# Decoder layer with product-key experts: order of ACT and PE within a step, the last unit's gathers, reused query weights, and the samples' values

## The reference, cut to what matters

```
mod = silu(c) @ w_ada + b_ada                  -> shift1, scale1, gate1, shift2, scale2, gate2
h   = rmsnorm(x) * (1 + scale1) + shift1
q, k, v, B, C, hc = split(h @ w_in)
x   = x + gate1 * (concat[window_attention(q, k, v), B * conv3(C * hc)] @ w_out)
h2  = rmsnorm(x) * (1 + scale2) + shift2
sc  = (h2 @ wq) . keys                         # 8 heads, two halves of 128 keys each
experts, gates = top 16 of the 16 x 16 sums, softmax
x   = x + gate2 * sum_k gates_k * gelu(peer_u[expert_k] . h2) * peer_v[expert_k]
y   = rmsnorm(x)
```

## Time and profile before

| | us |
|---|---|
| median of 3 runs | 3291.64 (3290.68 to 3293.53) |
| the profiled execution | 3288.59 |
| its span | 3286.6 |
| PE busy (matmuls) | 1843.0 |
| DVE busy | 2033.9 |
| ACT busy | 707.4 |
| POOL busy | 2063.0 |
| mean granted TensorE clock | 0.733 |

### The profile page before, as it was taken

How to read it: one execution, slowest core, us unless ns; L and a number is a source line. 1 busy time by engine, 2 the same in 40 slices (tenths; PEclk the granted TensorE clock), 3 DMA queues, 4 the chain that set the end, 5 groups by cost and what they waited for, 6 DMA issues and landing times.

```text
span 3286.6 us, 31584 instructions
## 1 busy us (share of the span) xinstructions
PE 1843.0 (56%) x9996; PEld 858.8 (26%) x9996; DVE 2033.9 (62%) x5142; ACT 707.4 (22%) x1967; POOL 2063.0 (63%) x2211
## 2 busy tenths in 40 slices
PE   5998478786467753364444444444444444545434
PEld 2456264343222310042112112111112111212110
DVE  3334845577687675466666666666666666666663
ACT  2121212212332131111222222222222222121111
POOL 1231656666576566557777777777777777777774
PEclk8999698998678875687676776766667676566665
DMA  8826999999999999999999999999999999999997
GB/s 305 264 96 223 351 387 369 410 389 380 364 384 388 348 371 406 408 352 404 410 409 409 409 409 406 408 403 407 401 409 404 405 407 407 405 406 404 404 407 264
DMA packets 396308, 1231.64 MB, mean 375 GB/s; under 512 B 54611, under 2 KB 107839, under 8 KB 392798
## 3 DMA queue, kind: packets, MB, share of 16 engines
q0 software_dynamic: 305728, 1109.92, 85.9%
q1 hardware_dynamic: 46314, 75.12, 6.5%
q10 hardware_dynamic: 44100, 44.59, 4.1%
HBM read 1214.45 MB, written 16.04 MB: 374 GB/s over the span
## 4 chain that ended last, share of the span: by engine, by line
POOL 28%; DMA 23%; PE 15%; DVE 14%; issue 12%; DVEq 2%; ACT 2%; ACTq 1%; SPq 1%; POOLq 0%
DMA arena<-in_peer_u,eid 15%; POOL arena L480 14%; POOL arena L491 14%; DVE arena L1491 8%; DMA arena<-in_peer_v,eid 8%; PE PS L784 3%; PE PS L662 3%; PE PS L607 2%; PE PS L624 2%; PE PS L636 2%; PE PS L712 1%; DVE arena L1480 1%; ACTq L904 1%; PE PS L674 1%; SPq L293 1%
## 5 line engine op out<-in xcount | busy, mean ns | idle before, releaser
L1491 DVE CUSTOM_DVE_ANT_0 arena<-arena,PS 128x1024 f32<-128x1024 f32 x1056 | 1243.3, 1215 | 475.8 <-DMA arena<-in_peer_u,eid 310.8
L784 PE MATMUL PS<-arena 128*32 128x512 f32 x4224 | 828.3, 925 | 1174.2 <-DMA arena<-in_peer_v,eid 1051.8
L480 POOL DMA_INDIRECT arena<-in_peer_u,eid x1056 | 997.9, 945 | 542.4 <-issue 284.5
L491 POOL DMA_INDIRECT arena<-in_peer_v,eid x1056 | 1002.6, 949 | 477.6 <-issue 299.1
L784 PEld LDWEIGHTS PS<-arena 128*32 128x32 f32 x4224 | 162.9, 145 | 1641.0 <-issue 1423.6
L1502 DVE SCALAR_TENSOR_TENSOR wgt<-gex,grec,gel 128x16 f32<-128x16 f32 x66 | 15.6, 237 | 404.7 <-ACT gel L1100 404.1
L1105 ACT ACTIVATE arena<-sel,wgt 128x32 f32<-128x32 f32 x1056 | 231.0, 307 | 40.0 <-DVE wgt L1502 40.0
L624 PE MATMUL PS<-arena 128*128 128x256 f32 (+1 forms) x576 | 172.2, 454 | 23.4 <-DVE arena L1334 21.4
L761 PEld LDWEIGHTS PS<-arena 128*128 128x128 f32 x1280 | 154.7, 201 | 46.7 <-issue 42.1
L761 PE MATMUL PS<-arena 128*128 128x128 f32 x1280 | 162.3, 287 | 3.3 <-ACT arena L1090 3.3
L1095 ACT ACTIVATE arena<-PS 128x256 f32<-128x256 f32 x42 | 16.1, 384 | 666.9 <-PE PS L772 666.9
(11 more groups left out here) (237 smaller groups left out, 1967.9 us busy)
## 6 DMA issues: line engine op xcount, KB each, us to landing
arena<-in_w_ada SPq DMA_DIRECT2D x24, 1024.0 KB, 8.1
arena<-in_peer_u,eid POOLq DMA_INDIRECT x1056, 9.3
arena<-in_peer_v,eid POOLq DMA_INDIRECT x1056
arena<-in_peer_wq ACTq DMA_DIRECT2D x13, 1024.0 KB, 6.5
arena<-in_peer_wq SPq DMA_DIRECT2D x4, 2048.0 KB, 42.2
arena<-in_w_in SPq DMA_DIRECT2D x14, 512.0 KB, 8.1
arena<-in_w_in ACTq DMA_DIRECT2D x14, 512.0 KB, 15.5
arena<-in_x_prompt ACTq DMA_DIRECT2D x8, 512.0 KB, 7.4
```

The lines of the kernel that those rows point to most:

```text
L480: po.indirect_dma_start(out=Ur[:, k % RING, :], out_offset=None, in_=a["peer_u"], in_offset=bass.IndirectOffsetOnAxis(ap=eid[m % 4][:, k:k ...
L491: po.indirect_dma_start(out=Vr[:, k % RING, :], out_offset=None, in_=a["peer_v"], in_offset=bass.IndirectOffsetOnAxis(ap=eid[m % 4][:, k:k ...
L784: last = mm(PS[j * GT:(j + 1) * GT, half, :], dsel[m % 2][:, k, :], Vr[:, k % RING, half * 512:(half + 1) * 512], start=m % 2 == 0 and q = ...
L1491: last = ve.tensor_tensor_reduce(out=Ur[:, k % RING, :], in0=Ur[:, k % RING, :], in1=hP, scale=1.0, scalar=0.0, op0=ALU.mult, op1=ALU.add, ...
```

## The change

Order on ACT: `selectors` loses its Gelu, which becomes the first thing in a step. The sample exponentials move behind the next piece's evacuation and `sample_soft2` one piece on. `store_mod` moves to positions 5 and 10. One root of a constant is computed ahead of the first norm. Order on PE: pieces i + 3 and i + 4 stand between quads 1 and 2, piece i + 5 between quads 2 and 3, none behind quad 3. Gathers: the last unit's quads 0 and 1 go into the ring of u rows, quads 2 and 3 into slots of the ring of v rows. Weights: heads 5 to 7, still in the buffers from the first tile, are the first three Q pieces, so three loads are left out. Samples' values (SD): the new rows' part for all eight samples is one matmul of 128 columns in place of eight of 16.

```diff
+            def gather_last(q):
+                po.wait_ge(s["dots_done"], (UNITS - 1) * NU + 6 + 2 * q)
+                for k in range(q * VB, (q + 1) * VB):
+                    po.indirect_dma_start(
+                        out=Ur[:, k % RING, :], out_offset=None, in_=a["peer_v"],
...
+                    ).then_inc(last_ld[q], 16)
+
-            for n in range(UNITS + 1):
+            for n in range(UNITS - 1):
...
+            for q in range(NV):
+                gather_u(UNITS - 1, 2 * q)
+                gather_u(UNITS - 1, 2 * q + 1)
+                if q == NV - 1:
+                    gather_last(0)
+                gather_v(UNITS - 2, q)
+            gather_last(1)
+            for q in (2, 3):
+                po.wait_ge(s["pv_done"], (UNITS - 2) * NV + q + 1)
...
                 if kind == "SD":
                     p = n * 64
+                    mm(PS[p:p + 64, 6, 0:NS * 16], vnat[0:NSAMP, PT, p:p + 64], PTn.rearrange("p n c -> p (n c)"), start=True, stop=False)
                     for m in range(NS):
-                        mm(PS[p:p + 64, 6, m * 16:(m + 1) * 16], cVn[:, m, p:p + 64], PTc[:, m, :], start=True, stop=False)
-                        last = mm(PS[p:p + 64, 6, m * 16:(m + 1) * 16], vnat[0:NSAMP, PT, p:p + 64], PTn[:, m, :], start=False, stop=True)
+                        last = mm(PS[p:p + 64, 6, m * 16:(m + 1) * 16], cVn[:, m, p:p + 64], PTc[:, m, :], start=False, stop=m == NS - 1)
...
                 if kind == "Q":
-                    pe.wait_ge(*take(wqA_ld, PH + n))
+                    pe.wait_ge(*take(wqA_ld, PH - 3 + n))
...
             def weigh(m, q):
                 pe.wait_ge(s["diag_ready"], m + 1)
-                pe.wait_ge(v_ld[q % VBUFS], 16 * VB * ((m * NV + q) // VBUFS + 1))
+                rows = Vr
+                if m < UNITS - 1:
+                    pe.wait_ge(v_ld[q % VBUFS], 16 * VB * ((m * NV + q) // VBUFS + 1))
+                elif q < 2:
+                    pe.wait_ge(last_ld[q], 16 * VB)
+                    rows = Ur
+                else:
+                    pe.wait_ge(v_ld[q % VBUFS], 16 * VB * (m * NV // VBUFS + 1))
...
                     weigh(n - 1, 1)
-                if i + 3 < last_i:
-                    piece(i + 3)
+                for q in (3, 4):
+                    if i + q < last_i:
+                        piece(i + q)
                 if 1 <= n <= UNITS:
                     weigh(n - 1, 2)
-                if i + 4 < last_i:
-                    piece(i + 4)
+                if i + 5 < last_i:
+                    piece(i + 5)
                 if FIRST <= n + 2 < UNITS:
                     scores(n + 2)
                 if 1 <= n <= UNITS:
                     weigh(n - 1, 3)
-                if i + 5 < last_i:
-                    piece(i + 5)
...
                 last.then_inc(s["piece_ev"], 1)
+                if i and PIECES[i - 1][0] == "SB":
+                    ac.wait_ge(s["sm_done"], PIECES[i - 1][1] + 1)
+                    act_(SS, SS, ACT.Exp)
+                    act_(ses[:, :], ses[:, :], ACT.Exp).then_inc(s["se_done"], 1)
...
                     if n + 3 < PH:
-                        load_wqA(PH + n + 3)
+                        load_wqA(PH + n)
...
-                if pos in (4, 8):
-                    store_mod(pos // 4)
+                if pos in (5, 10):
+                    store_mod(pos // 5)
...
+            act_(sqw[:, :], epsb[:, :], ACT.Sqrt)
             first_squares(0)
...
-                load_wqA(h + 3)
+                if h + 3 < PH:
+                    load_wqA(h + 3)
...
+            def gelu(m):
+                ac.wait_ge(s["dots_done"], (m + 1) * NU)
+                act_(gel[:, m % 2, :], act[:, m % 2, :], ACT.Gelu).then_inc(s["gelu_done"], 1)
+
             def selectors(m):
                 par = m % 2
-                ac.wait_ge(s["dots_done"], (m + 1) * NU)
-                act_(gel[:, par, :], act[:, par, :], ACT.Gelu).then_inc(s["gelu_done"], 1)
...
+                if 1 <= n <= UNITS:
+                    gelu(n - 1)
                 left = n >= 2 and i - 1 < last_i
...
-                if before == "SB":
-                    sample_soft2(m)
+                if i >= 2 and PIECES[i - 2][0] == "SB":
+                    sample_soft2(PIECES[i - 2][1])
```

More of the change, by code:

```diff
@@ L219, in build @@
         wgt = sb("wgt", [128, 2, TOPK])
-        rin, epsb = sb("rin", [128, 5]), sb("epsb", [128, 1])
+        rin, epsb, sqw = sb("rin", [128, 5]), sb("epsb", [128, 1]), sb("sqw", [128, 1])
         tickv = sb("tickv", [128, 4])
@@ L246, in build @@
         v_ld = [sem(f"v_ld{i}") for i in range(VBUFS)]
+        last_ld = [sem(f"last_ld{i}") for i in range(2)]
         block = ctx.enter_context(nc.Block())
@@ L494, in gather_v @@
                     ).then_inc(v_ld[b % VBUFS], 16)
-            for n in range(UNITS + 1):
+            def gather_last(q):
[3 more added lines that the diff above has]
+                        out=Ur[:, k % RING, :], out_offset=None, in_=a["peer_v"],
+                        in_offset=bass.IndirectOffsetOnAxis(ap=eid[(UNITS - 1) % 4][:, k:k + 1], axis=0),
+                    ).then_inc(last_ld[q], 16)
+            for n in range(UNITS - 1):
                 for q in range(NV):
@@ L502, in _ @@
                         gather_v(n - 1, q)
+            for q in range(NV):
[7 more added lines that the diff above has]
+                po.wait_ge(s["pv_done"], (UNITS - 2) * NV + q + 1)
+                for k in range(q * VB, (q + 1) * VB):
+                    po.indirect_dma_start(
+                        out=Vr[:, k % RING, :], out_offset=None, in_=a["peer_v"],
+                        in_offset=bass.IndirectOffsetOnAxis(ap=eid[(UNITS - 1) % 4][:, k:k + 1], axis=0),
+                    ).then_inc(v_ld[q % VBUFS], 16)
         @block.tensor
@@ L607, in piece @@
                                 last = mm(PS[:, 6 + n % 2, half * 256 + (t - 1) * 128:half * 256 + t * 128],
-                                          wqA[(PH + n) % 3][:, k, half * 128:(half + 1) * 128], (h2T[1] if t == 1 else h2T2)[:, k, :],
+                                          wqA[(PH - 3 + n) % 3][:, k, half * 128:(half + 1) * 128], (h2T[1] if t == 1 else h2T2)[:, k, :],
                                           start=k == 0, stop=k == KT - 1)
@@ L783, in weigh @@
                         j = k % 4
-                        last = mm(PS[j * GT:(j + 1) * GT, half, :], dsel[m % 2][:, k, :], Vr[:, k % RING, half * 512:(half + 1) * 512],
+                        last = mm(PS[j * GT:(j + 1) * GT, half, :], dsel[m % 2][:, k, :], rows[:, k % RING, half * 512:(half + 1) * 512],
                                   start=m % 2 == 0 and q == 0, stop=m % 2 == 1 and q == NV - 1)
@@ L943, in piece @@
                 if kind == "SB":
-                    ac.wait_ge(s["sm_done"], n + 1)
-                    act_(SS, SS, ACT.Exp)
-                    act_(ses[:, :], ses[:, :], ACT.Exp).then_inc(s["se_done"], 1)
                     return
@@ L980, in piece @@
                 if kind == "Q":
-                    last = act_(qA12[:, 2 * n:2 * n + 2, :], PS[:, 6 + n % 2, :].rearrange("p (a b) -> p a b", a=2), ACT.Copy)
+                    last = act_(qA12[:, 2 * ((PH - 3 + n) % PH):2 * ((PH - 3 + n) % PH) + 2, :], PS[:, 6 + n % 2, :].rearrange("p (a b) -> p a b", a=2), ACT.Copy)
                 if kind == "W":
```

## The result

| | before, us | after, us |
|---|---|---|
| median of 4 runs | 3291.16 | 3247.84 (3242.39 to 3251.76) |
| the profiled execution | 3288.59 | 3242.39 |
| its span | 3286.6 | 3240.6 |
| first gather issued | 287.87 | 274.95 |
| first gather of unit 24 | 1478.2 | 1439.8 |

The ratio is 0.9873, with a 95% interval of 0.9859 to 0.9887: 43.3 us faster, where 31.3 were forecast. The profiled execution after is the fastest of its four, so the 46.0 us between the two spans are some 3 us more than the medians give. The gathers' start times sort these 46.0: 12.9 us before the first gather (forecast 13.7), 25.6 between the first gather and unit 24 (10), none from there to the last unit (1711.6 us against 1711.5), 7.6 in the tail (7.6).

What follows compares the result with a forecast made beforehand. DMA was taken to bound the kernel after the start: time to first gather, DMA work, holes, tail. Start 13.7, middle 10 and tail 7.6 sum to 31.3 us, off the median 3291.64 giving 3260; range 3241 to 3278.

Steps and rivals of the forecast that it cites:

- the middle gives much: Rival for 400 to 1500 us: stretches at DMA share 0.93 with long Gelu waits yield 25 us, 3245; chance 0.11.
- The bound: From 1500 to 3230 us gathers fill DMA, share 1.02 at 407 GB/s, and nothing else makes that stage shorter.
- The start: Chain before the first gather: P0's gap, slow group, SD, groups behind it and root save 13.7 us, passed through.
- What is late next? DVE: Start, after P0's gap goes: DVE's sample_soft2 would end at 151, covered by PE work until near 153.
- SD: Samples' values on PE: 18 matmul records for 32 save 3.5 us, plus 1 us from slow groups behind.
- the rival that put 8 us on them: Rival at the first gathers: the three wq loads held them, so 8 us come on top, 3252; chance 0.02.
- The middle: From 400 to 1500 us: early Gelu and new piece order fill DMA holes, 10 us, kept between -5 and +25.
- I take a quarter of the bound: Middle: of the 43 us of DMA holes over 400 to 1500 us, 10 us were taken as gain.
- The slower rival: PE steps 4 to 17: a piece ahead of the fourth quad holds the ring; 3312 at 3 us per step; chance 0.05.
- The mark set for "wrong": Profile sign that the forecast fails: POOL waiting for PE more than 172 us.
- The second mark: Profile sign that the forecast fails: new holes between 500 and 1200 us.
- The tail: Last unit: quads 0 and 1 in the u ring bring the last gather earlier, 7.6 us, kept between 6 and 9.

Runs made afterwards that it cites:

- e6: The changed kernel with the modulation stores back at positions 4 and 8; 3243.50 us.
- e9: The changed kernel with the 4 MB of w_out loaded behind the weights of position 14, on a slower chip; ratio 0.9824 to the kernel before.
- e8: The changed kernel with the 16 matmuls of each SD piece back; 3249.73 us.
- e5: The changed kernel with the three left-out wq loads of 1 MB made again; 3247.38 us, ratio 0.9878.
- e1: The changed kernel with the Gelu back behind the piece's copy, spread and take_y, on a slower chip; ratio 0.9867 to the kernel before.
- g1: The kernel before with only the new order of pieces on PE, on a slower chip; ratio 0.9895 to the kernel before.

## Why the prediction was right, and where it was off

The measured 3247.84 us lie inside the stated range, but nearer to the rival "the middle gives much" (3245, chance 0.11) than to the forecast of 3260 (0.55). The mechanisms hold in the main; the sizes of start and tail came out near by luck, as follows, and the middle was put too low.

**The bound.** Right: the long stage moved by 0.1 us in 1711, and every gain came before or behind it. From 1478 to 3190 us DVE's wait for the Gelu fell from 196.8 to 22.4 us, which gave nothing, as forecast for the full stage.

**The start**, 13.7 us forecast, 12.9 measured, by other terms, and in part by luck: 2.0 of the 12.9 lie ahead of every edit, and 2.5 more in a slow group that the same code does not always have. The gap and the slow work behind it went (8.6 us, forecast 7.9). "What is late next? DVE" was wrong: DVE was covered, but the weights of position 11 were late: 4.29 us of wait and 1.4 in a slow group. The prediction had looked at SP's queue behind the moved store, and not at what SP had issued ahead, with PE now 8 us earlier; e6 and e9 show it from both sides. SD was forecast at 3.5 us and 1 for the groups; it gives 3.0 (e8) to 6.2 (before against after), depending on whether the group behind the second piece runs slow. Its own rows give more than forecast, 2.1 and 2.6 us, since the 18 records follow each other every 0.08 us where the 32 did every 0.11; but of the first piece 1.0 us was lost to PE's wait for ACT behind it. The 3.9 us of the forecast had 0.36 us of that wait in them. The root gave 1.3, as its row said; the 2.66 us that the Trainium skill gives for a switch (*ScalarE: Activation LUTs*, *What ACT_TABLE_LOAD costs*) would have been twice that, and the measurement decides. wq's loads gave nothing, as costed (e5); the rival that put 8 us on them fell.

**The middle**, 10 us forecast, 25.6 measured: this term was mis-sized. The step that failed is "I take a quarter of the bound". The bound, 43 us from the DMA share, held on this chip (on the slower one the two edits brought 51). What was missing is the wait that answers to it: POOL waited 98.3 us for dots in the stretch, some two thirds of it right behind a long wait of DVE for the Gelu. The prediction listed DVE's 404.1 us and POOL's wait for PE, and not POOL's for DVE. Both edits act on that same wait, so it fell to 35.4, and of the 63 us less 26 came back as waits for PE and 10 as waits for indices. Some 27 us remain, beside 25.6 us of time. The rival "the middle gives much", 25 us and 3245, is the one that came true.

**The slower rival** did not. POOL's wait for PE rose, as its mechanism says (141.5 to 167.4 us; 63 to 78 us more by the order alone on the slower chips), but by less than the wait for dots fell. The mark set for "wrong", more than 172 us of waits for PE over the whole trace, was passed (186.7) in a kernel that is faster: waits of POOL for one ring say nothing without those for the other. The second mark, new holes between 500 and 1200 us, did not show: the DMA share rose in each of the stretches 500 to 700, 700 to 900, 900 to 1050 and 1050 to 1200 (1.01, 1.01, 1.00, 0.94 before; 1.04, 1.03, 1.02, 0.96 after).

**The tail**, 7.6 forecast and measured, and the equality is luck. The last quad came 5.9 us earlier, not 7.6: POOL waited 4.34 us for the sixth dot pair and then 2.70 for the weighing of unit 64, as kept in the bounds. The other 1.7 us are the clock at which PE weighs the last quad, 1.92 us where it took 3.64, and most traces with the new tail don't have them. Over all runs the tail is worth 6.7 to 6.8 us.

## What to carry to other kernels

When one in-order queue feeds two rings, add up its waits for both before an order is changed, and look for the engine that holds the ring's consumer: two edits that act on the same waits overlap, here some 35 us each and 51 together. When a gap is removed from the leading engine, look at what every queue had issued ahead by then, not only behind the moved instruction. Split a gain by milestones in the trace, such as the first gather of a unit, and keep apart the stretches that the edit cannot touch: their scatter can be larger than the effect. And put the first milestone behind the last wait that stands ahead of every edit: a forecast that is met by the difference of two profiles can be met by their scatter.

## What was not expected of the hardware

The same kernel takes 3287 us on one chip and 3574 on two others: the long stage runs at 406 GB/s with a DMA share of 1.02 on the first and at 365 to 369 with 0.97 on the others. Over 1400 us of that stage, in the changed kernel's kin e1:

```profile
1700.00:3100.00 1400.00, 623.07 (x3608) 255.63 (x3608) 838.00 (x2202) 263.66 (x759) 913.97 (x974) 0.66 0.97 369
```

POOL issues each gather in the same time there (0.94 us) but waits more: in these 1400 us 185.4 us in 61 waits, at v gathers, that the profile puts down to no engine of this core (`remote`), where the changed kernel on the first chip has no such wait. What slows the transfers was not traced. And the clock of TensorE fell over gaps of a few us in both kernels: behind the new wait for weights the group runs at a mean granted clock of 0.70, between the levels of 2.4 GHz (1.0) and 1.2 GHz (0.5), the window being

```profile
155.20:160.00 4.80, 4.80 (x17) 2.49 (x18) 1.57 (x3) 1.04 (x5) 0.00 (x0) 0.70 1.06 304
```

so a removed wait was worth about 1.4 us more than its length at P0 and at position 11 (groups of 4.49 and 4.46 us against 3.06). But the level differs between runs of the same code: the group behind the second SD takes 5.57 us in the kernel before and 3.06 in g1, and the last quad's weighing 1.92 or 3.2 to 3.6.
